# Eight modulation blocks on VectorE, ten landing places, and a different order of the first transfers

## The reference, cut to what matters

```python
s_lat, s_ctx = silu(c), silu(c_ctx)
mod   = s_lat @ ada_w + ada_b          # 6 parts of 2048: sh1, sc1, g1, sh2, sc2, g2
mod_c = s_ctx @ ada_w + ada_b          # only csh1 and csc1 are used
h  = rmsnorm(x) * (1 + sc1) + sh1;  hc = rmsnorm(ctx) * (1 + csc1) + csh1
x  = x + g1 * (y @ w_out)
x  = x + g2 * conv_gated_mlp(rmsnorm(x) * (1 + sc2) + sh2)
```

## Time and profile before

| | us |
|---|---|
| median of 3 runs | 3231.94 (3230.67 to 3234.11) |
| the profiled execution, its own time | 3229.23 |
| its span in the trace | 3227.4 |
| PE busy in the span | 3089.8 |
| DVE, ACT, POOL busy | 1917.2, 1415.5, 244.4 |

### The profile page before, as it was taken

One profiled execution on the slowest core, in us unless ns is written; L12 is line 12 of the kernel. 1 busy time (PEld: TensorE's weight loads), 2 busy tenths in 40 slices (PEclk: granted clock), 3 DMA queues, 4 the chain that ended last, 5 costly groups with the idle time before them and its releaser, 6 DMA issues.

```text
span 3227.4 us, 54438 instructions
## 1 busy us (share of the span) xinstructions
PE 3089.8 (96%) x22670; PEld 2696.5 (84%) x22670; DVE 1917.2 (59%) x2598; ACT 1415.5 (44%) x1994; POOL 244.4 (8%) x203
## 2 busy tenths in 40 slices
PE   7999989899999999999999999999998999999998
PEld 6898978787888888888788889988877888888887
DVE  5475763543755785555555565345667666666666
ACT  4343442433544573444434454343425445444443
POOL 1100321020100110000000230010001000000002
PEclk9999999999999999999999999999999999999999
DMA  6554555546644666777777777763434566656654
GB/s 213 177 159 132 156 177 198 189 157 207 228 153 148 205 191 191 230 253 241 256 246 253 249 242 239 252 187 115 159 104 147 173 205 182 187 180 194 187 177 146
DMA packets 535783, 620.07 MB, mean 192 GB/s; under 512 B 19451, under 2 KB 459926, under 8 KB 534177
## 3 DMA queue, kind: packets, MB, share of 16 engines
q1 hardware_dynamic: 527008, 586.51, 57.7%
q0 software_dynamic: 3344, 23.78, 2.1%
q10 hardware_dynamic: 5184, 6.29, 0.6%
HBM read 608.12 MB, written 8.39 MB: 191 GB/s over the span
## 4 chain that ended last, share of the span: by engine, by line
PE 78%; DVE 4%; ACT 2%; DMA 2%; issue 1%; POOL 0%; SPq 0%; ACTq 0%; DVEq 0%; POOLq 0%
PE psum L591 35%; PE psum L592 18%; PE psum L563 3%; PE psum L566 3%; PE psum L565 3%; PE psum L691 3%; PE psum L1749 2%; PE psum L625 2%; PE psum L627 2%; PE psum L628 2%; DVE wlo L520 1%; DMA wraw<-in_ffn_w 1%; PE psum L675 1%; PE psum L2398 0%; PE psum L1940 0%
## 5 line engine op out<-in xcount | busy, mean ns | idle before, releaser
L513 ACT ACTIVATE whi<-wraw 128x1024 fp32r<-128x1024 f32 (+1 forms) x948 | 977.7, 1033 | 1203.7 <-PE psum L592 455.4
L520 DVE TENSOR_TENSOR wlo<-wraw,whi 128x1024 fp32r<-128x1024 f32 (+1 forms) x948 | 1150.8, 1226 | 559.6 <-ACT whi L513 552.6
L591 PE MATMUL psum<-g,whi 128*128 128x512 f32 x2816 | 1000.9, 397 | 15.8 <-issue 8.2
L591 PE MATMUL psum<-h,whi 128*128 128x512 f32 x2240 | 793.4, 396 | 5.0 <-DVE h L2037 2.4
L592 PE MATMUL psum<-g,wlo 128*128 128x256 f32 x2816 | 788.3, 280 | 0.0
L591 PEld LDWEIGHTS psum<-g,whi 128*128 128x128 f32 x2816 | 530.5, 188 | 162.9 <-issue 25.9
L592 PE MATMUL psum<-h,wlo 128*128 128x256 f32 x2240 | 633.6, 283 | 0.0
L592 PEld LDWEIGHTS psum<-g,wlo 128*128 128x128 f32 x2816 | 530.7, 188 | 0.5
L591 PEld LDWEIGHTS psum<-h,whi 128*128 128x128 f32 x2240 | 421.2, 188 | 122.9 <-issue 21.9
L592 PEld LDWEIGHTS psum<-h,wlo 128*128 128x128 f32 x2240 | 421.7, 188 | 0.2
L563 PE MATMUL psum<-h,whi 128*128 128x256 f32 x1040 | 304.3, 293 | 35.1 <-DVE h L896 22.0
(11 more groups left out here) (468 smaller groups left out, 3368.2 us busy)
## 6 DMA issues: line engine op xcount, KB each, us to landing
wraw<-in_ffn_w SPq DMA_DIRECT2D x256, 512.0 KB, 6.7
wraw<-in_w_in SPq DMA_DIRECT2D x204, 512.0 KB, 4.7
wraw<-in_ada_w SPq DMA_DIRECT2D x192, 512.0 KB, 4.8
wraw<-in_ffn_w_up SPq DMA_DIRECT2D x160, 512.0 KB, 4.5
wraw<-in_w_out SPq DMA_DIRECT2D x64, 512.0 KB, 4.5
wraw<-in_ffn_w_down SPq DMA_DIRECT2D x64, 512.0 KB, 4.6
wraw<-in_xattn_wk SPq DMA_DIRECT2D x32, 512.0 KB, 4.5
wraw<-in_xattn_wv SPq DMA_DIRECT2D x32, 512.0 KB, 4.6
```

The lines of the kernel that those rows point to most:

```text
L513: e.activation(high(i), view(WRAW[i % NR], i), ACT.Copy).then_inc(*hi.up(i))
L520: e.tensor_tensor(low(i), view(WRAW[i % NR], i), high(i).bitcast(F32), SUB).then_inc(*lo.up(i))
L591: e.matmul(both_of(g, j), w_hi[:, kk, s:s + 128], X[:, k, :], start=k == 0, stop=False, skip_group_check=True)
```

## The change

1. Of the modulation's blocks 8 to 23, the eight in `BY_PE` stay on PE. The other eight (8, 9, 12, 13, 16, 17, 20, 21) are summed by DVE (`rows_v`): each landed 128 x 512 half of a chunk is multiplied by its column of silu(c), one number per partition, and added to a running sum in `ACM` (which lies in `CX`, the context's copy). After the last chunk DVE adds the two halves, and PE sums over partitions with ones in the same four tiny matmuls (`gather_p`). Only silu(c) is used for them; blocks 8 and up are not used for the context.
2. `ada2` is now blocks 8 to 21, one chunk after every 2 of dn0 to dn3 and two after every 4 of up1 to up3; with this the summed blocks fall beside dn0, dn1, dn2 and dn3 and PE's blocks beside up1, up2 and up3. `ada3` is blocks 22 and 23, two chunks after every 8. The copy, gather and bias of the last block move behind the start of the next stage's product; POOL's fills of `HY` wait for it.
3. NR is 10. `WLO[i]` is the same memory as `WRAW[i]`: DVE writes the low part over the landed chunk. SP may overwrite an ordinary or a PE block's chunk when PE is done with it, and a summed one when DVE has added it.
4. `mats` is asked for on ACT's queue behind x, POOL asks for the filters when the last part of x has landed, and the waits for `mats` on PE and DVE move into the side work of the first product, one step ahead of the norm's sums.

```diff
-NR = 6
+NR = 10
...
-WF = 4
+WF = 2
...
-WC = 4
+WC = 8
...
-NA2 = 20
+BY_PE = (10, 11, 14, 15, 18, 19, 22, 23)
...
-def weave(main, extra, per):
+def weave(main, extra, per, times=1):
...
-            for other in islice(extra, 2):
+            for other in islice(extra, times):
...
-        WRAW = [new(f"wraw{i}", [P, CS]) for i in range(NR)]
+        landing_places, place = scope()
+        WRAW = [place(f"wraw{i}", [P, CS]) for i in range(NR)]
+        landing_places.close()
+        WLO = [new(f"wlo{i}", [P, CS], F32R) for i in range(NR)]
         WHI = [new(f"whi{i}", [P, CS], F32R) for i in range(NH)]
-        WLO = [new(f"wlo{i}", [P, CS], F32R) for i in range(NH)]
...
-        MO4 = TM[:, 2:4, :].rearrange("p a t -> p (a t)")
...
+        ACM = CX[:, 0:8, :].rearrange("p a t -> p (a t)").rearrange("p (b c n) -> p b c n", b=2, c=2)
...
-        MO2 = FT[:, 0:2, :].rearrange("p a t -> p (a t)")
...
+                    if n >= NA0 and n not in BY_PE:
+                        summed[len(chunks) - 1] = n, k // 2, PL[name][-1][1]
...
-        woven = plan_ada("ada2", NA0, NA2)
+        woven = plan_ada("ada2", NA0, 22)
         for i in range(4):
-            made(weave(plan(f"up{i}", "ffn_w1", 0, 16, cols(2048 * i, 2048 * i + 2048, 256), "v"), woven if i else iter(()), WF))
-            made(weave(plan(f"dn{i}", "ffn_w2", 16 * i, 16, cols(0, 2048, 256), "v"), woven if i else iter(()), WF))
-        woven = plan_ada("ada3", NA2, 24)
+            made(weave(plan(f"up{i}", "ffn_w1", 0, 16, cols(2048 * i, 2048 * i + 2048, 256), "v"), woven if i else iter(()), 2 * WF, 2))
+            made(weave(plan(f"dn{i}", "ffn_w2", 16 * i, 16, cols(0, 2048, 256), "v"), woven, WF))
+        woven = plan_ada("ada3", 22, 24)
         for name, c in (("k2c", 1024), ("v2c", 2048), ("k2x", 1024), ("v2x", 2048)):
-            made(weave(plan(name, "w_in_2", 0, 16, cols(c, c + 1024, 256), "a"), woven, WC))
+            made(weave(plan(name, "w_in_2", 0, 16, cols(c, c + 1024, 256), "a"), woven, WC, 2))
...
+        def raw(i):
+            return view(WRAW[i % NR], i)
+
+
         def low(i):
-            return view(WLO[nth[i] % NH], i)
+            return view(WLO[i % NR], i)
 
...
-                e.activation(high(i), view(WRAW[i % NR], i), ACT.Copy).then_inc(*hi.up(i))
+                e.activation(high(i), raw(i), ACT.Copy).then_inc(*hi.up(i))
 
         def split_lo(e, i):
+            if i in summed:
+                rows_v(e, *summed[i])
             if i not in plain:
                 e.wait_ge(*hi.at(i))
-                if nth[i] >= NH:
-                    e.wait_ge(*mm.at("chunk", halved[nth[i] - NH]))
-                e.tensor_tensor(low(i), view(WRAW[i % NR], i), high(i).bitcast(F32), SUB).then_inc(*lo.up(i))
+                e.tensor_tensor(low(i), raw(i), high(i).bitcast(F32), SUB).then_inc(*lo.up(i))
...
+            e.dma_start(MT[:, :], A_["mats"]).then_inc(*d_mt.up("all"))
...
-            return 6 + n % 2 if NA0 <= n < NA2 else 1 + 2 * (n % 2)
+            return 6 + n % 2 if n >= NA0 else 1 + 2 * (n % 2)
+
+        def side_by_side(e, n, i, before, k0):
+            for k in range(k0 - 2, k0 + 2):
+                q = k % 4
+                x = e.matmul(PSUM[32 * q:32 * q + 32, ada_bank(n), :], SF[:, k:k + 16, :].rearrange("p k m -> p (k m)"),
+                             raw(i if q > 1 else before)[:, q % 2, :], start=k < 4, stop=k >= 12)
+            ends = [("chunk", before), ("chunk", i)]
+            x.then_inc(*mm.up(*(ends + [("ada", n)] if k0 == 14 else ends)))
...
+        def rows_v(e, n, ci, ids):
+            a, (i, k0, m), before = ACM[:, n % 2, :, :], ids[ci], ids[ci - 1][0]
+            if ci == 0 and n > NA0 + 1:
+                e.wait_ge(*ada.p.at("mod", n - 2))
+            landed(e, i)
+            if ci:
+                e.wait_ge(*ada.v.at("sum", before))
+            for kk in range(2):
+                w, by = raw(i)[:, kk, :], SF[:, k0 + kk, 0:1]
+                if ci == 0:
+                    x = e.tensor_scalar(a[:, kk, :], w, by, None, MUL)
+                else:
+                    x = e.scalar_tensor_tensor(a[:, kk, :], w, by, a[:, kk, :], MUL, ADD)
+            x.then_inc(*ada.v.up(("sum", i)))
+            if ci == 7:
+                e.wait_ge(*ada.v.now())
+                e.tensor_tensor(a[:, 0, :], a[:, 0, :], a[:, 1, :], ADD).then_inc(*ada.v.up(("acc", n)))
+
+        def mod_v(e, name, lo_to, weight=None):
+            for n, ids in PL[name]:
+                for ci, (i, k0, m) in enumerate(ids):
+                    lo_to(e, reach(i, 2))
+                    if ci == 6 and n > NA0:
+                        modulation_v(e, n - 1)
+                    yield weight
+
+        def copied_a(e, n, acc):
+            e.wait_ge(*mm.at("ada", n))
+            e.wait_ge(*ada.p.at("mod", n - 2))
+            e.activation(acc[:, n % 2, 0, :], PSUM[:, ada_bank(n), :], ACT.Copy).then_inc(*ada.a.up(("mo", n)))
+
+        def mod_a(e, name, acc, hi_to, weight=None):
+            for n, ids in PL[name]:
+                for ci, (i, k0, m) in enumerate(ids):
+                    hi_to(e, reach(i, 3))
+                    if ci == 2 and n - 1 in BY_PE:
+                        copied_a(e, n - 1, acc)
+                    yield weight
+
+        def gather_p(e, n, acc):
+            e.wait_ge(*(ada.a.at("mo", n) if n in BY_PE else ada.v.at("acc", n)))
+            for j in range(4):
+                x = e.matmul(PSUM[:, ada_bank(n), 2 * j:2 * j + 2], acc[:, n % 2, 0, 128 * j:128 * j + 128],
+                             CB[:, :] if n in BY_PE else ones[:, 0:2], start=True, stop=True)
+            x.then_inc(*ada.p.up(("mod", n)))
+
+        def mod_p(e, name, acc, weight=None):
+            for n, ids in PL[name]:
+                for ci, (i, k0, m) in enumerate(ids):
+                    if ci == 4 and n > NA0:
+                        gather_p(e, n - 1, acc)
+                    if n in BY_PE:
+                        if ci == 0:
+                            e.wait_ge(*ada.v.at("mod", n - 2))
+                        landed(e, i)
+                        if ci % 2:
+                            side_by_side(e, n, i, ids[ci - 1][0], k0)
+                    yield weight
...
         def sync(e):
             e.dma_start(PK[:, :], A_["pack"]).then_inc(*d_pk.up("all"))
-            e.dma_start(MT[:, :], A_["mats"]).then_inc(*d_mt.up("all"))
             for i in range(len(chunks)):
                 j = i - NR
-                if j in plain:
+                if j in summed:
+                    e.wait_ge(*ada.v.at("sum", j))
+                elif j >= 0:
                     e.wait_ge(*mm.at("chunk", j))
-                elif j >= 0:
-                    e.wait_ge(*lo.at(j))
-                e.dma_start(view(WRAW[i % NR], i), chunks[i][0]).then_inc(*w_in[i % NR].up())
+                e.dma_start(raw(i), chunks[i][0]).then_inc(*w_in[i % NR].up())
...
         def tensor(e):
-            e.wait_ge(*d_mt.at("all"))
-            side = Side(sums_p(e, fn, TM1, False, 0.3), idle(1), spectrum_p(e))
+            side = Side(then(lambda e: e.wait_ge(*d_mt.at("all")), e), sums_p(e, fn, TM1, False, 0.3), idle(1), spectrum_p(e))
...
-            extra = ada_p(e, "ada2", MO4, WA)
+            extra = mod_p(e, "ada2", ACM, WA)
...
-                                  here, WF))
+                                  here, 2 * WF, 2))
...
                 side.beside(weave(gemm_wide_p(e, PL[f"dn{i}"], HX, lambda e, k: e.wait_ge(*ff1.v.at("lo", i, k))),
-                                  here, WF))
-                if i == 3:
-                    made(extra)
+                                  extra, WF))
...
-            e.wait_ge(*ada.v.at("mod", 23))
-            side = Side()
+            side = Side(idle(2), then(lambda e: gather_p(e, 23, ACM), e))
...
-            ada_first_v(e)
...
-            side = Side(sums_v(e, fn, RS1[:, :], None, 0.3), then(fn.ended, e), spectrum_v(e))
+            side = Side(then(ada_first_v, e), sums_v(e, fn, RS1[:, :], None, 0.3), then(fn.ended, e), spectrum_v(e))
...
-            side = Side()
+            side = Side(idle(5), then(lambda e: modulation_v(e, 23), e))
...
-            side = Side(sums_a(e, fn, X0, TM1, RS1[:, :], None, 0.3), then(fn.ended, e), spectrum_a(e))
+            side = Side(idle(1), sums_a(e, fn, X0, TM1, RS1[:, :], None, 0.3), then(fn.ended, e), spectrum_a(e))
...
-            side = Side()
+            side = Side(then(lambda e: copied_a(e, 23, ACM), e))
...
         def gpsimd(e):
             ada_first_g(e)
+            e.wait_ge(*d_x0[3].at("all"))
             load_filters(e)
...
-            inn.ended(e)
+            e.wait_ge(*ada.v.at("mod", 23))
```

More of the change, by code:

```diff
@@ L396, in build @@
         fills = count("fills")
-        chunks, blocks_made, plain = [], [], set()
+        chunks, blocks_made, plain, summed = [], [], set(), {}
         def chunk(w, k0, k, m, c0, n):
@@ L2616, in vector @@
             extra = ada_v(e, "ada1", lo_to, WA)
[L2617 to L2618 removed]
```

(2 more changed lines are left out.)

83 lines of the change are left out of this document (37 added, 46 removed).

## The result

After the change the median is 3153.65 us (3146.51 to 3156.39, 4 runs) against 3231.31 us (3224.83 to 3234.11, 4 runs) of the kernel before beside it: a ratio of 0.9754 (0.973 to 0.9778), 77.7 us faster. The forecast was 3176 us with a range from 3158 to 3203, so the sign was right and the size wrong: 22 us too little, and 4 us outside the range.

What follows compares the result with a forecast made beforehand. PE, busy 3089.8 of 3227.4 us, was taken to bound nearly everywhere. Terms -34.6 + 3 - 12 - 3 - 7.5 - 2 = -56.1 took the profiled 3229.2 to 3173.1; the median, 2.7 above, gave 3176 us, range 3158 to 3203.

Steps and rivals of the forecast that it cites:

- The RWKV term (-12): RWKV part: ten places and low parts in place free ACT's late chunks; -12 us, half of the bounds 0 and -25.
- Rival C: RWKV part gives back all 25 us, with the start at its best: 3161 us; chance 0.13.
- rival B: RWKV part: ACT's waits only change name, from late chunks to PE's release of `WHI`; no gain there, 3188 us; chance 0.22.
- The group's price (1.08): Modulation: each group of four matmuls costs PE 1.08 us; 32 groups leave PE, -34.6 us.
- DVE's stalls (+3): Down products, mainly dn3: all stalls from DVE's added sums cost +3 us, between nothing and 20.
- The waits of the earlier trace: 1319 to 1914 us: PE's waits from late chunks (2.4 us) and the copy ending `ada2` (0.7) go; -3 us.
- Rival D: dn3: DVE and POOL shut each other out, costing 20 us instead of 3: 3193 us; chance 0.10.
- rival F: Down products: DVE becomes the bound, needing over 3.3 us per summed chunk; slower, up to 3355 us; chance 0.03.
- Rival E: Down products: transfers become the bound if 249 GB/s is all they get; 45 us, 3221 us; chance 0.03.
- The start: Kernel's start: chunk 0 lands at 10 us, first matmul at 14.5; -7.5 us, between -4 and -10.
- PE's wait of 2.0 us for POOL's squares: First product's side work: norm's sums move two chunks later, so this wait ends; -2 us, 0 at the least.

Runs made afterwards that it cites:

- experiment 1: Kernel before with nothing but ten landing places and the low parts written in place: 3199.01 us, ratio 0.9899.
- experiment 7: Kernel after with eight landing places instead of ten: 3154.83 us.
- experiments 2 and 6: 2: kernel before with only DVE's sums of eight blocks and new chunk order, 3191.74 us; 6: kernel after with all sixteen blocks on DVE, 3114.45 us.
- Experiment 5: Kernel after with each summed chunk added a second time by DVE: 3172.81 us, ratio 0.9819.
- Experiment 10: Two versions of the kernel after: POOL asks for the filters at once, 3158.49 us; SP asks for `mats` ahead of chunk 0, 3156.69 us.

## Why the prediction was wrong, point by point

**The RWKV term (-12) was mis-sized; it is what failed first.** The prediction took the transfers on the chain, 25 us, as the bound, and half of it as the term. Measured are 22.3 us in that part together with the rest, inside the bounds, and 27.8 for the places alone, beyond them. PE's idle time fell to the 25 us that the prediction named. Three things were missed.

There was no row behind the half: nothing in the profile named work that would hold the RWKV steps for as long as the transfers had, and none did.

The bound was short of one transfer. The chain of the kernel before has a seventh in the same stretch:

```profile
777.84 6.10 DMA wraw<-in_w_out
```

With it the bound is 31 us, and the matmuls from 780.3 to 809.1 us around its end, 28.8 us, take 24.5 in the kernel after.

And PE's busy time was taken as fixed, though 6.7 us of the gain (9.6 in experiment 1) were the clock's; the earlier trace rows had shown a mean of 0.96 in 390 to 800 us, and the prediction quoted it without giving it a price. In the traces with six places the sum by windows is 15.3 to 18.7 us in this part (four executions), with ten 5.1 to 11.9 (eight).

The mechanism, that a chunk in a full place comes late, ACT waits for it and the RWKV steps wait behind ACT, is borne out where most of the gain is (the 302 matmuls of experiment 7). As a measure of the gain ACT's waits mislead: with eight places 120 of 144 us are still there, and so are 18.6 us of `xattn` transfers on the chain (5.94, 6.78 and 5.84), and the part is as short as with ten. Rival C, that all 25 us come back, was the nearest, at a chance of 0.13; rival B is refuted, though its renamed waits are there: ACT's largest wait for PE in the RWKV steps grew from 44.2 us (L1626) to 77.4 (L1698, the same line), while PE's idle time fell.

**The group's price (1.08) was mis-sized.** It left out the stretched pair behind most groups: 1.19, as the timeline after and experiments 2 and 6 show (36.7 to 38.6 us for 32 groups, 34.6 forecast). The sign of it, the L591 of 0.50 us in the earlier trace rows, was at hand.

**DVE's stalls (+3) were nothing.** The sums cost 0.80 us per half chunk instead of 0.7, and PE idles 1.3 us in 943. In dn1 and dn2 DVE is busy 78% where the prediction had 82: its own work is 5.9 us per four chunks there, not 6.5. The waits of the earlier trace rows are gone, as forecast (-3).

**Rival D's mechanism is there, its cost is refuted.** DVE does slow down beside POOL. Groups of DVE in the kernel after, 1380 to 1480 us, where POOL is idle, and then 1755 to 1845, where it is busy 40 of 90 us:

```profile
L527 DVE TENSOR_TENSOR wlo<-wraw,whi 128x1024 fp32r<-128x1024 f32 x35 | 41.6, 1218 | 3.2 <-ACT whi L520 3.2
L754 DVE SCALAR_TENSOR_TENSOR cx<-wraw,sf,cx 128x512 f32<-128x512 f32 x22 | 15.4, 743 | 0.0
```
```profile
L527 DVE TENSOR_TENSOR wlo<-wraw,whi 128x1024 fp32r<-128x1024 f32 x32 | 44.4, 1420 | 1.5 <-ACT whi L520 1.5
L754 DVE SCALAR_TENSOR_TENSOR cx<-wraw,sf,cx 128x512 f32<-128x512 f32 x26 | 24.9, 995 | 0.0
```

That is 32 x 0.20 + 26 x 0.25 = 13 us of DVE's time, and DVE was still idle 8 of 90 us. The means mix two kinds. Inside the second window the 15 low parts that no instruction of POOL overlaps take 1.21 us, as in the first, and of the 12 that POOL overlaps throughout ten take 1.75 to 1.76, with POOL stretched too (two low parts, then one of POOL's additions beside them):

```profile
1783.68 3.44 DVE L527 TENSOR_TENSOR wlo<-wraw,whi 128x1024 fp32r<-128x1024 f32 x2
```
```profile
1786.00 1.72 POOL L1957 TENSOR_TENSOR acc<-acc,sq 128x256 f32<-128x256 f32 x1
```

POOL's addition takes 0.73 us at the least, so a pair takes 1.76 us beside each other and 1.94 one after the other: the two hardly overlap. By the Trainium skill, SBUF — State Buffer, section "Who interferes with whom", the sums are of the kind that POOL can hold up; the rows agree with that. The sum of rival D went wrong in taking POOL's 39.6 us of the earlier trace rows as its work. These are 27 additions, about 20 us at 0.73 each (an estimate from these rows); with DVE's 44.5 + 24 that is 88 of 88 us, not 108. Experiment 5 shows the point where the cover ends. That is rival F's mechanism, at work in one product of four. The prediction had let the cover end at 2.4 us per summed chunk and F begin at 3.3; at 3.1 (four times 0.78) dn1 and dn2 are just covered, and dn3, where a chunk takes 3.6 (four times 0.89), is not.

**Rival E is refuted:** the DMA engines moved 276 to 279 GB/s in the down products, where 249 were feared to be the limit.

**The start.** The forecast -7.5 was 8.1 at the first matmul, 14.5 us forecast and 13.9 measured. PE's wait of 2.0 us for POOL's squares is gone too, as forecast; but its wait for the squares of the memory's norm, before 326 us, grew from 1.8 to 3.3. Up to the norm's sums PE's idle time falls by 8.9 us (37.9 to 29.0), near the forecast of 9.5, and PE's busy time takes 1.3 back (295.8 and 297.1 us; the sum by windows is 6.9 and 8.5), which leaves about the 7.5 of the table. The prediction took chunk 0's landing at 10 us by bytes in front of it, and it was 9.4. By the Trainium skill, DMA: Bandwidth & Descriptors, section "Queues, rings and completion order", the queues take turns, and by that the prediction had it near 8; the measured 9.4 lies nearer to the 9.7 of all bytes in a row. Experiment 10 speaks for the turns in part: 0.2 MB ahead of chunk 0 on its own queue cost 2.4 us, though they are only 0.7 us at 306 GB/s. By two queues in turn it would be twice that, about 1.3 us by estimate, so the turns alone don't give the 2.4.

**The sum.** Of the 22 us, 10.3 are the RWKV part, 6.7 the part with the modulation (up to 4 the groups, 3 the stalls) and 1.7 the rest, less 2 of the start. The other 5.4 are between profiled execution and median: the prediction added 2.7 us, and after the change it was 2.7 the other way. That last share is chance: 2.7 us above the profiled execution, as before the change, the median would have been 3159.1, inside the range by 1 us.

## What to carry to other kernels

Where PE has gaps and the granted clock of the stretch is below its upper level, closing the gaps can give more than their length: here 0.43 to 0.52 us of busy time on top of each us of idle time (6.7 to 15.6, 9.6 to 18.3). How much of it comes back varies from one execution to the next, so compare several. Before counting an engine's waits as a gain, look whether the engine that bounds the time idles in the same stretch: of ACT's 144 us, 90 could go or stay without a trace in the time. Price a group of unlike instructions up to the start of the second ordinary pair behind it, not of the first. A busy time that was measured beside another engine can hold that engine's delays: take the shortest record as the work. And a bound that a chain of waits gives is no reason to take its half: ask which row would keep the other half, and if there is none, take the whole.

## What the runs showed of the hardware

The clock's part was not expected: 6.9 us of the RWKV part's gain, and in the part with the modulation, where it stays at its upper level in the kernel before and after, 3.4 us of loss in experiment 5, where PE had 14.6 us of gaps. The first pair of wide matmuls behind a group of 32-column ones is 0.11 us longer each time. DVE beside a busy POOL was slowed by 17% (1.42 for 1.22 us) on the low parts and by 34% (0.99 for 0.74) on the sums in the mean; fully beside it a low part takes 1.76 and a sum up to 1.23, and POOL's own addition up to 1.72 instead of 0.73. Nothing there comes near the single 2.61 us of the earlier trace rows. DVE's additions that read one operand from PSUM weren't slowed (0.42 us in both windows). And two orders of the first transfers that each cost chunk 0 under 3.5 us cost 7.5 together.
